# Norm waits moved to the block that needs them, modulation units regrouped, and a convolution moved from GpSimd to VectorE in a two-layer diffusion trunk

## The reference, cut to what matters

```python
for l in range(DEPTH):
    sh1, sc1, g1, sh2, sc2, g2 = split(silu(c) @ mod_w[l] + mod_b[l], 6)
    h = modulate(rms_norm(x, norm1_g[l]), sh1, sc1)
    o, oc = even_mixer(...) if l % 2 == 0 else odd_mixer(...)
    x = x + g1 * o
    x = x + g2 * swiglu(modulate(rms_norm(x, norm2_g[l]), sh2, sc2), ffn_w_in[l], ffn_w_out[l])
```

## Time and profile before

| what | value |
|---|---|
| three executions | 1261.22, 1265.18 and 2963.65 us (median 1265.18 us) |
| the profiled execution's own time | 1263.81 us |
| its span | 1262.0 us |
| its mean granted TensorE clock | 0.979 |

### The profile page before, as it was taken

One profiled execution on the slowest core, in us unless ns is written; L12 is line 12 of the kernel. 1 busy time (PEld: TensorE's weight loads), 2 busy tenths in 40 slices (PEclk: granted clock), 3 DMA queues, 4 the chain that ended last, 5 costly groups with the idle time before them and its releaser, 6 DMA issues.

```text
span 1262.0 us, 17678 instructions
## 1 busy us (share of the span) xinstructions
PE 1183.2 (94%) x7274; PEld 952.4 (75%) x7274; DVE 714.0 (57%) x1078; ACT 482.9 (38%) x624; POOL 72.2 (6%) x74
## 2 busy tenths in 40 slices
PE   4799999899899999999999899899779998999998
PEld 3477766687588888888887578796445698999998
DVE  2689998742623233333332668757878645555554
ACT  3413235741433322222222433352447635554332
POOL 0200000000000000000000003801600000000000
PEclk9799999999999999999999999899889999999999
DMA  8735344035452223432226543242005254546532
GB/s 313 276 134 200 126 172 171 2 102 198 157 178 90 68 68 107 133 101 87 75 75 217 183 134 100 67 147 89 1 1 195 74 167 133 171 155 190 196 127 97
DMA packets 119883, 166.45 MB, mean 132 GB/s; under 512 B 4509, under 2 KB 112391, under 8 KB 113543
## 3 DMA queue, kind: packets, MB, share of 16 engines
q1 hardware_dynamic: 119382, 164.99, 39.2%
q10 hardware_dynamic: 433, 0.51, 0.1%
HBM read 164.44 MB, written 1.05 MB: 131 GB/s over the span
## 4 chain that ended last, share of the span: by engine, by line
PE 79%; DVE 15%; ACT 2%; issue 2%; DMA 2%; SPq 0%; POOL 0%; ACTq 0%; DVEq 0%
PE acc L1753 21%; PE acc L1754 21%; PE acc L1755 21%; PE pmod L1704 3%; DVE w_lo L528 2%; DVE Y L1146 2%; PE p L1674 1%; PE acc L1769 1%; PE acc L1770 1%; PE acc L1771 1%; PE acc L1674 1%; PE acc L2268 1%; PE p L2213 1%; PE p L2294 1%; DMA raw<-in_mod_w 1%
## 5 line engine op out<-in xcount | busy, mean ns | idle before, releaser
L528 DVE TENSOR_TENSOR w_lo<-raw,w_hi 128x2048 fp32r<-128x2048 f32 (+3 forms) x118 | 252.4, 2139 | 290.7 <-ACT w_hi L525 290.5
L525 ACT ACTIVATE w_hi<-raw 128x2048 fp32r<-128x2048 f32 (+3 forms) x118 | 210.6, 1784 | 448.7 <-PE acc L1755 419.9
L1753 PE MATMUL acc<-Hhi,w_hi 128*128 128x512 f32 (+1 forms) x992 | 342.1, 345 | 12.7 <-DVE w_lo L528 7.0
L1754 PE MATMUL acc<-Hlo,w_hi 128*128 128x512 f32 (+1 forms) x992 | 339.5, 342 | 0.0
L1755 PE MATMUL acc<-Hhi,w_lo 128*128 128x512 f32 (+1 forms) x992 | 339.3, 342 | 0.0
L1753 PEld LDWEIGHTS acc<-Hhi,w_hi 128*128 128x128 f32 x992 | 190.5, 192 | 38.2 <-issue 15.9
L1755 PEld LDWEIGHTS acc<-Hhi,w_lo 128*128 128x128 f32 x992 | 190.5, 192 | 20.9
L1754 PEld LDWEIGHTS acc<-Hlo,w_hi 128*128 128x128 f32 x992 | 190.6, 192 | 20.4
L1753 PE MATMUL acc<-hid_hi,w_hi 128*128 128x512 f32 (+1 forms) x448 | 157.7, 352 | 0.7 <-DVE hid_lo L1342 0.7
L1755 PE MATMUL acc<-hid_hi,w_lo 128*128 128x512 f32 (+1 forms) x448 | 155.8, 348 | 0.0
L1754 PE MATMUL acc<-hid_lo,w_hi 128*128 128x512 f32 (+1 forms) x448 | 155.7, 348 | 0.0
(11 more groups left out here) (289 smaller groups left out, 1445.9 us busy)
## 6 DMA issues: line engine op xcount, KB each, us to landing
raw<-in_mod_w SPq DMA_DIRECT2D x48, 1024.0 KB, 5.0
raw<-in_ffn_w_in SPq DMA_DIRECT2D x44, 1024.0 KB, 5.1
raw<-in_od_w_in SPq DMA_DIRECT2D x15, 1024.0 KB, 5.6
raw<-in_ffn_w_out SPq DMA_DIRECT2D x16, 768.0 KB, 4.7
raw<-in_ev_w_in SPq DMA_DIRECT2D x10, 1024.0 KB, 7.9
raw<-in_ffn_w_out SPq DMA_DIRECT2D x16, 640.0 KB, 4.1
raw<-in_od_w_out SPq DMA_DIRECT2D x8, 1024.0 KB, 5.6
raw<-in_ev_w_out SPq DMA_DIRECT2D x8, 768.0 KB, 6.3
```

Source lines behind the costliest of these rows:

```text
L525: nc.scalar.activation(w_hi[:, w % 2, 0:n], raw[:, r % RAW_SLOTS, 0:n], ACT.Copy).then_inc(hi_split, 1)
L528: nc.vector.tensor_tensor(w_lo[:, w % 2, 0:n], raw[:, r % RAW_SLOTS, 0:n], w_hi[:, w % 2, 0:n].bitcast(F32), ALU.subtract).then_inc(lo_spl ...
L1753: mm(outs[m], hi[:, j, cols], xh, start=(first and j == 0), stop=False)
L1754: mm(outs[m], hi[:, j, cols], xl, start=False, stop=False)
```

## The change

1. `MOD_EARLY` is 3, and `MOD_WAIT` names the other five units: units 3, 4 and 5 are what norms 1 and 2 run in `square_sums`; units 6 and 7 run in `paired_product`, between k-tile 3 of the first weight block and k-tile 0 of the second. The stream has units 3, 4, 5 ahead of the second weight block and 6, 7 behind it; two units fewer stand between the blocks of the product ahead of each norm.
2. `first_ready` is gone. `paired_product` calls `enter(b, j0)` ahead of each quarter, and `second_weights` waits there for the second block's low split, behind the units 6 and 7. Norm 3 has no units and gets the moved wait alone.
3. The convolution of tiles 8 to 11 leaves GpSimd. `conv_pair` is the code that stood in the loop; it now also runs for pair 4 (tiles 8, 9) at n = 6 and for pair 5 (tiles 10, 11, latents alone) at n = 8, ahead of the keys' rotation.
4. The softplus moves from n = 6 to n = 7.

```diff
         for k, item in enumerate(ev_out_blocks[3:]):
-            stream += [("mod", 1, 0, k), item]
+            stream += [("mod", 1, 0, k)] * (k < MOD_EARLY) + [item]
...
                 for p_ in range(nt // 2):
                     for side in range(2):
                         stream.append(("w", ffn_in[l], 0, KD, side * FFN + P * t0 + BC * p_, BC))
-                    if l == 0 and half == 0 and p_ == 0:
-                        stream.extend(("mod", 1, 0, k) for k in range(MOD_EARLY, KD))
+                        if l == 0 and half == 0 and p_ == 0:
+                            stream.extend(("mod", 1, 0, k) for k in MOD_WAIT[side])
...
         for n, (kind, src, col) in enumerate(blocksC):
             stream.append(("w", src, 0, KD, col, 32 if kind == "dt" else BC))
-            if n == 1:
-                stream += [("mod", 1, 1, k) for k in range(MOD_EARLY, KD)]
+            if n < 2:
+                stream += [("mod", 1, 1, k) for k in MOD_WAIT[n]]
...
                     if alone:
-                        load(r)
-                        load(r + 1)
-                        r, w = r + 2, w + 2
-                        while stream[r][0] == "mod":
+                        for _ in range(2):
                             load(r)
-                            r += 1
+                            r, w = r + 1, w + 1
+                            while stream[r][0] == "mod":
+                                load(r)
+                                r += 1
                         if l == 0:
                             sp.wait_ge(mod_used, 4 * KD)
                             sp.wait_ge(lo_split, w)
...
-            for i in range(8, XBC_T):
-                pool.wait_ge(read_act, C_READS[x_block(i // 2)][1])
-                o, src = conv_C(i)
-                z = ptapC[:, 0:2, :] if i < 10 else ptapC[:, 0, :]
-                step(nc.gpsimd.tensor_scalar(o, src(0), cvw(0, i), vec[:, CVB + i:CVB + i + 1], ALU.mult, ALU.add))
-                for tap in range(1, S_CONV):
-                    step(nc.gpsimd.tensor_scalar(z, src(tap), cvw(tap, i), 0.0, ALU.mult, ALU.add))
-                    ins = nc.gpsimd.tensor_tensor(o, o, z, ALU.add)
-                    if tap < S_CONV - 1:
-                        step(ins)
-                ins.then_inc(s("conv_C_pool"), 1)
-                pool.wait_ge(s("conv_C_pool"), i - 7)
...
-                    act.wait_ge(s("conv_C_dve") if i < 8 else s("conv_C_pool"), i + 1 if i < 8 else i - 7)
+                    act.wait_ge(s("conv_C_dve"), i + 1)
...
                 if n == 12:
                     silu_xc(range(8))
-                    act.wait_ge(s("conv_C_pool"), 4)
...
+            def conv_pair(j):
+
...
+                for tap in range(S_CONV):
+                    for i in (2 * j, 2 * j + 1):
+                        o, src = conv_C(i)
+                        if tap == 0:
+                            ins = V_.tensor_scalar(o, src(0), cvw(0, i), vec[:, CVB + i:CVB + i + 1], ALU.mult, ALU.add)
+                        else:
+                            ins = V_.scalar_tensor_tensor(out=o, in0=src(tap), scalar=cvw(tap, i), in1=o, op0=ALU.mult,
+                                                          op1=ALU.add)
+                        if tap == S_CONV - 1:
+                            ins.then_inc(s("conv_C_dve"), 1)
+                        else:
+                            step(ins)
...
-                if n == 6:
+                if n == 7:
                     softplus()
                 if n == 8:
+                    conv_pair(5)
                     dve.wait_ge(s("aux_done"), 6)
                     rope(Kc[:, 0:LAT], p6[:, 0:LAT], modc[:, 0:LAT], cst("cosC"), cst("sinC"))
...
-                if n in (1, 3, 4, 5):
-
...
+                if n in (1, 3, 4, 5, 6):
+                    conv_pair((1, 3, 4, 5, 6).index(n))
...
-            def paired_product(blocks, rhs, ready):
+            def paired_product(blocks, rhs, ready, enter):
 
                 for j0 in (0, KD // 2):
-                    for outs, hi, lo, width in blocks:
+                    for b, (outs, hi, lo, width) in enumerate(blocks):
+                        enter(b, j0)
                         for j in range(j0, j0 + KD // 2):
                             ready(j)
                             xh, xl = rhs(j)
@@ -1934,12 +1922,22 @@
                     for f in range(q - 3, KD if q == 7 else q - 1):
...
                 if q == 7:
-                    fill = {1: range(3 * KD + MOD_EARLY, 4 * KD), 2: range(4 * KD + MOD_EARLY, 5 * KD)}.get(n, ())
+                    fill = [KD * (n + 2) + k for k in MOD_WAIT[0]] if n < 3 else []
                     for m in fill[:1]:
                         mod_unit(m)
                     spread_roots(n, t)
                     for m in fill[1:]:
                         mod_unit(m)
+
+            def second_weights(n, w):
+
+                def enter(b, j0):
+                    if b == 1 and j0 == 0:
+                        for m in [KD * (n + 2) + k for k in MOD_WAIT[1]] if n < 3 else ():
+                            mod_unit(m)
+                        pe.wait_ge(lo_split, w + 2)
+
+                return enter
...
-                if n >= 3:
+                if 3 <= n < 3 + MOD_EARLY:
                     mod_unit(3 * KD + n - 3)
...
-                        both_ready = stream_in(2 * l + 1)
-
-                        def first_ready(j, w=w):
-
-                            both_ready(j)
-                            if j == KD // 2 - 1:
-                                pe.wait_ge(lo_split, w + 2)
-
                         paired_product([([acc[:, 2 * side + m, 0:t] for m in range(2)], *split_block(w + side, KD), P)
-                                        for side in range(2)], H(t), first_ready)
+                                        for side in range(2)], H(t), stream_in(2 * l + 1), second_weights(2 * l + 1, w))
...
-
-                    def first_ready(j):
-
-                        stream_in(2)(j)
-                        if j == KD // 2 - 1:
-                            pe.wait_ge(lo_split, w + 2)
-
                     paired_product([([acc[:, m, :] for m in range(2)], *split_block(w, KD), P),
-                                    ([acc[:, 2 + m, :] for m in range(2)], *split_block(w + 1, KD), P)], H(T), first_ready)
+                                    ([acc[:, 2 + m, :] for m in range(2)], *split_block(w + 1, KD), P)], H(T),
+                                   stream_in(2), second_weights(2, w))
...
-MOD_EARLY = 5
+MOD_EARLY = 3
+
+MOD_WAIT = ((3, 4, 5), (6, 7))
```

More of the change, by code:

```diff
@@ L245, in build_trunk @@
         Z = view("Z", [KD, LAT], r_misc + 16384)
-        ptapC = view("ptapC", [2, LAT], r_misc + 16384)
         vT = view("vT", [T], r_misc + 18432)
@@ L1433, in xw @@
                                  head_cols(DW[:, n, :]), ALU.mult).then_inc(s("xw_ready"), 1)
+            def conv_pair(j):
+                dve.wait_ge(read_act, C_READS[x_block(j)][1])
+                dve.wait_ge(s("pads_C"), 2)
+                for tap in range(S_CONV):
[10 more added lines that the diff above has]
+                            step(ins)
             norm(2, T, C_IN + 1)
@@ L1486, in _ @@
                     ins.then_inc(s("k2_ready"), 1)
-                if n in (1, 3, 4, 5):
-                    j = (1, 3, 4, 5).index(n)
-                    dve.wait_ge(read_act, C_READS[x_block(j)][1])
-                    dve.wait_ge(s("pads_C"), 2)
-                    for tap in range(S_CONV):
-                        for i in (2 * j, 2 * j + 1):
-                            o, src = conv_C(i)
-                            if tap == 0:
-                                ins = V_.tensor_scalar(o, src(0), cvw(0, i), vec[:, CVB + i:CVB + i + 1], ALU.mult,
-                                                       ALU.add)
-                            else:
-                                ins = V_.scalar_tensor_tensor(out=o, in0=src(tap), scalar=cvw(tap, i), in1=o,
-                                                              op0=ALU.mult, op1=ALU.add)
-                            if tap == S_CONV - 1:
-                                ins.then_inc(s("conv_C_dve"), 1)
-                            else:
-                                step(ins)
+                if n in (1, 3, 4, 5, 6):
+                    conv_pair((1, 3, 4, 5, 6).index(n))
                 if 9 <= n <= 12:
```

## The result

The changed kernel took 1250.49 us (median of 1249.94 to 1251.31 us); the kernel before, run beside it, 1263.93 us (a median of four, one of them the execution of 2963.65 us). The ratio is 0.9899 with a 95% interval of 0.9879 to 0.9918: 10 to 15 us faster, about 1%. The profiled execution took 1250.01 us with a span of 1248.2 us at a mean granted clock of 0.985. The forecast was 1252 us, in a range of 1246 to 1260.

What follows compares the result with a forecast made beforehand. TensorE, busy 94% of the span, was taken to bound the kernel. Gains of 4.4 + 0.8 + 0.6 + 5.7 = 11.5 us off the profiled 1263.81 us gave 1252 us, range 1246 to 1260.

Steps and rivals of the forecast that it cites:

- The units in the product: Ahead of norms 1 and 2: four units leave the row of blocks, 1.1 us each, 4.4 us gained, bounds 3.8 and 4.8.
- The pair in norms 1 and 2: Units 6 and 7 fill the wait ahead of the second weight block: 0.4 us gained per norm, 0.8 together.
- (a): Rival, more comes out: no wait ahead of block 10 and no slow spell in norm 2, 1248.8 us; chance 0.14.
- Norm 3: No units there; the second block follows k-tile 2 without its low-split wait: 0.6 us gained, bounds 0 and 1.1.
- Convolution and softplus: Layer 1's input projection: block 8's 5.02 us wait goes, block 10 starts 5.7 us earlier; bounds +7.6 and -7.
- the softplus: On VectorE at n = 7: falls from 14.0 to 5.7 us without GpSimd beside it; upper bound 14.0.
- keys: On VectorE in layer 1's projection: 9.1 us falls to 7.5 us as four copies get shorter.
- the wait ahead of block 10: TensorE in layer 1's projection: block 10 waits 1.9 us for VectorE, the next thing that is late.
- (b): Rival, softplus stays long at 14.0 us: stalls only move, 1.7 us gained in the projection, 1262.1 us; chance 0.08.
- (c): Rival, second weight block lands late in norms 1 and 2, holding ScalarE and TensorE: 1267.9 us; chance 0.03.
- (d): Rival, units gain nothing: they cost in the norm what they cost between blocks, 4.4 us given back, 1256.7 us; chance 0.13.
- The prediction's warning: The 1.9 us wait ahead of block 10 could make a low-clock spell as long as block 8's, 8.2 against 5.9 us.

Runs made afterwards that it cites:

- e6: Changed kernel with five units ahead in the product again, three ahead of the first block's k-tile 3 side, none behind k-tile 3: 1252.88 us, ratio 0.9927 to before.
- e3: Kernel before with only the softplus moved from n = 6 to n = 7, convolution left on GpSimd: 1257.46 us, ratio 0.9948 to before.
- e4: Kernel before with GpSimd's convolution of tiles 8 to 11 replaced by zero fills, softplus left at n = 6: 1256.20 us, ratio 0.9929.
- e9: Kernel before with GpSimd's convolution of tiles 8 to 11 begun only after the softplus, still at n = 6: 1257.37 us, ratio 0.9965.
- e5: Changed kernel with the convolution of tiles 10 and 11 moved from n = 8 to n = 10: 1246.51 us, ratio 0.9879 to before.
- e7: Changed kernel with four units ahead of the second weight block in the stream and one behind k-tile 3: 1259.81 us, ratio 0.9970 to before.
- e2: Kernel before with parts 1 and 2 of the change alone, convolution and softplus as before: 1255.97 us, ratio 0.9934.
- e11: Changed kernel with the softplus back at n = 6, convolution kept on VectorE: 1252.53 us, ratio 0.9924 to before.
- e8: e5 with two units ahead in the product, three at the first block's side and three behind k-tile 3: 1249.79 us, ratio 0.9890 to before.

## Why the prediction was right

The forecast gain was 11.5 us. The two profiles differ by 13.8 us, the medians by 13.4 us in the first run and 11.3 in the second. The terms:

**The units in the product: 4.4 forecast, 4.0 measured** (2.07 and 1.94). One costs 1.0 us there, two in a row 0.96 each, so the lower bound was nearer.

**The pair in norms 1 and 2: 0.8 forecast, 0.30 in norm 1 and about as much of norm 2's 1.77.** The other 1.5 us of norm 2 are the spell at 1.2 GHz that isn't there after. It stood in the prediction as a bound and in rival (a), not in the sum. In norm 2 it was in all five profiles with the old layout and in none of the seven with at least two units behind k-tile 3 and the load in time. The term that was mis-sized is this one: a spell that stands behind a wait that goes was left to the bounds. That "two units are run in it and 0.4 us gained" holds, but e6 shows the two parts: 1.56 us from the moved wait, 1.26 back for the pair. The pair is worth having because it costs 2.0 in the product.

**Norm 3: 0.6 forecast, 0.79 measured**, with no wait for a low split at k-tile 3 any longer.

**Convolution and softplus: 5.7 forecast, 5.70 measured.** That it fits so closely is luck: the same code takes 4.5 to 5.8 us off this stretch over five profiles. The steps fit each by itself: the softplus 5.7 forecast, 5.3 measured; pair 5 4.4 and 4.9; keys 7.5 and 7.1; the wait ahead of block 10 1.9 and 2.1; no wait ahead of block 8 or 9. What was wrong is what these steps were credited to. The prediction ran the softplus at 14 us only with the pairs on VectorE (rival (b), 1.7 us gained). It never asked what the move of the softplus alone would do, and that is 5.4 us in the same stretch (e3). That instructions of VectorE with two SBUF inputs contend with GpSimd is the rule of the page "SBUF — State Buffer", section "Who interferes with whom" of the Trainium skill, and e3, e4 and e9 agree with it. The same section names copies and `tensor_scalar` among those that can contend: here a `tensor_scalar` took 1.32 us instead of 0.22 in the kernel before, though 0.21 in e3, and the keys' copies 4.47 us instead of 1.73 in e9. The reciprocal, with one input, isn't stretched (0.95 us).

**Not foreseen:** 0.9 us in the scan, which no part brings by itself. The same kernel run again took 1.7 us more there at a lower granted clock, so it is no result.

**Rivals.** (a) had 0.14: its half in norm 2 came, its other half (no wait ahead of block 10) not; e5 shows that it was to be had, at 2.25 us in the stretch for the 1.9 priced. (b) fell with the softplus's 5.3 us. (c) was held off by a thin margin: one more unit ahead of the load costs e7 6 to 9 us. (d) fell with e2 and e6, but it held a part of the truth: of the 2.0 us that a pair costs in the product, 1.26 come back in the norm.

## What to carry to other kernels

Before moving work off an engine to relieve a chain, try the order: what the bound engine waits for goes ahead of long work that nobody wants soon, and here that alone gave nearly as much as both edits (5.4 us against 5.7 at the same clock) with the slow chain left slow. Where a wait of TensorE that goes has a spell at the low clock right behind it in the timeline, count the spell too (1.5 us behind the 2.2 us: in norm 2 in all five profiles, in norm 1 in two of them). Put added work where the engine's timeline shows idle time *after* the move, not before it. A wait belongs at the first instruction that reads what it waits for, and work that must be done somewhere on the bound engine fills the gap that is left, as long as it doesn't keep a buffer that the next load needs (e7). And a stretch read from one profile is worth no more than its clock: look at the granted clock before a difference of 1 us is believed.

## What was unexpected of the hardware

The spells at 1.2 GHz are not all brought by waits. Behind 5.0 us (before, e2) and 3.5 us (e11) ahead of block 8 there is one, behind none there is none. But block 10 begins or runs at the low clock in 13 of the 14 profiles (all but e5), whether it waited 2.4 us or not at all. In e4, e7 and e8 the clock fell while TensorE was at work, during the 28 narrow matmuls (128x16) ahead of it, or right behind them:

```profile
808.07 3.93 PE L2147 MATMUL pmod<-dts,const 128*128 128x16 f32 x28
811.84 0.56 PE L1745 MATMUL acc<-Hhi,w_hi 128*128 128x256 f32 x1
```

That is e4, where nothing held block 10 (the 28 took 3.61 us in e8 and 3.57 in e7); in e5 the same 28 took 3.19 us and the block followed at the full clock, with the same work ahead. What decides between the two stays open. The prediction's warning that the new wait could make a spell in block 10 can't be shown either way: it was there before the change (7.41 us) and after it (7.39).

The disturbance between VectorE and GpSimd goes both ways. In e9 GpSimd's first multiplication, which took 0.91 us in the kernel before, began beside a low split on VectorE and took 2.66:

```profile
789.70 2.66 POOL L617 TENSOR_SCALAR XC<-XB,vec 128x512 f32<-128x512 f32 x1 [64.06 <-DVE dts L1402]
```
